# Value units read as halves of the contraction: 512-column matmuls into two banks, and another unit order in the memory layers

## The reference, cut to what matters

```python
# layer 0: vg is the gate input of the gated MLP, 512 columns
q, k, v, iq, ik, iw, u, vg = split_cols(h @ ab_w_in[e], AB_SPLITS)
y_b = gmlp_spatial_gate(gelu(u), gelu(vg), ...)
# layer 1: i are the values (1024 columns), gate the output gate (1024)
q, f, i, gate = split_cols(h @ c_w_in[o_i], C_SPLITS)
o = rms_norm(hgrn2(q, f, i, lb_all[l]), c_out_norm[o_i])
y = (o * silu(gate)) @ c_w_out[o_i]
# layers 2 and 3: q, k, v of 768 columns each, qm of 256
proj = xn @ w_in
self_out = attention(q, k, v);  mem_out = memory_attention(qm, mk, mv)
h = h + concat(self_out, mem_out) @ w_out[i]
```

## Time and profile before

| | us |
|---|---|
| median of 3 runs (lowest, highest) | 1290.58 (1290.05, 1291.75) |
| the profiled execution's own time | 1290.27 |
| its span, first to last instruction | 1288.5 |
| PE busy | 1272.3 |
| PE weight loads busy | 1127.0 |
| DVE busy | 991.9 |
| ACT busy | 751.0 |

### The profile page before, as it was taken

One profiled execution on the slowest core, in us unless ns is written; L12 is line 12 of the kernel. 1 busy time (PEld: TensorE's weight loads), 2 busy tenths in 40 slices (PEclk: granted clock), 3 DMA queues, 4 the chain that ended last, 5 costly groups with the idle time before them and its releaser, 6 DMA issues.

```text
span 1288.5 us, 21452 instructions
## 1 busy us (share of the span) xinstructions
PE 1272.3 (99%) x8114; PEld 1127.0 (87%) x8114; DVE 991.9 (77%) x1470; ACT 751.0 (58%) x1095; POOL 17.8 (1%) x34
## 2 busy tenths in 40 slices
PE   8999999999999999999999999999999999999998
PEld 7898888888999988888889888888889997888886
DVE  5898798888788778899987766777776675866665
ACT  5465665555877657776656656544445555644443
POOL 2000000000000001000000000000000000000000
PEclk9999999999999999999999999999999999999999
DMA  9554655556534347566546443655564444556551
GB/s 320 198 164 134 196 196 187 182 187 194 155 108 136 127 151 242 176 211 200 184 128 196 132 133 130 209 186 193 195 194 158 155 145 134 180 196 195 190 185 49
DMA packets 168918, 223.19 MB, mean 173 GB/s; under 512 B 5240, under 2 KB 150784, under 8 KB 168720
## 3 DMA queue, kind: packets, MB, share of 16 engines
q1 hardware_dynamic: 166480, 216.04, 51.4%
q0 software_dynamic: 1936, 5.54, 1.3%
q10 hardware_dynamic: 432, 0.64, 0.1%
HBM read 221.15 MB, written 1.06 MB: 172 GB/s over the span
## 4 chain that ended last, share of the span: by engine, by line
PE 86%; DVE 7%; ACT 3%; issue 2%; DMA 1%; DVEq 0%; SPq 0%; ACTq 0%
PE bank L547 21%; PE bank L385 16%; PE bank L386 15%; PE bank L387 15%; PE bank L550 11%; DVE wlow L1563 2%; PE bank L872 2%; ACT whigh L1105 1%; PE bank L641 1%; PE bank L677 1%; PE bank L663 1%; PE bank L462 1%; DMA raw<-in_ab_w_in 1%; DMA raw<-in_ffn_w_down 1%; DVE conv_b L1700 1%
## 5 line engine op out<-in xcount | busy, mean ns | idle before, releaser
L1563 DVE TENSOR_TENSOR wlow<-raw,whigh 128x2048 fp32r<-128x2048 f32 (+1 forms) x203 | 462.4, 2281 | 137.6 <-ACT whigh L1105 137.1
L1105 ACT ACTIVATE whigh<-raw 128x2048 fp32r<-128x2048 f32 x202 | 386.1, 1912 | 230.5 <-PE bank L387 148.4
L547 PE MATMUL bank<-xn,whigh 128*128 128x512 f32 x1312 | 327.9, 392 | 0.0
L547 PEld LDWEIGHTS bank<-xn,whigh 128*128 128x128 f32 x1312 | 238.2, 189 | 44.1
L550 PEld LDWEIGHTS bank<-xn,wlow 128*128 128x128 f32 x1312 | 179.0, 190 | 12.8
L550 PE MATMUL bank<-xn,wlow 128*128 128x256 f32 x1312 | 182.9, 282 | 0.0
L385 PE MATMUL bank<-xn,whigh 128*128 128x256 f32 (+1 forms) x560 | 161.8, 289 | 0.6 <-DVE wlow L1563 0.6
L386 PE MATMUL bank<-xn,whigh 128*128 128x256 f32 (+1 forms) x560 | 158.3, 283 | 0.0
L387 PE MATMUL bank<-xn,wlow 128*128 128x256 f32 (+1 forms) x560 | 158.2, 283 | 0.0
L385 PE MATMUL bank<-whigh,g_high 128*128 128x512 f32 x354 | 138.7, 392 | 1.7 <-DVE g_low L1759 1.0
L386 PE MATMUL bank<-wlow,g_high 128*128 128x512 f32 x354 | 137.8, 389 | 0.0
(11 more groups left out here) (292 smaller groups left out, 1756.1 us busy)
## 6 DMA issues: line engine op xcount, KB each, us to landing
raw<-in_ffn_w_up SPq DMA_DIRECT2D x44, 1024.0 KB, 5.1
raw<-in_w_gate_up SPq DMA_DIRECT2D x44, 1024.0 KB, 5.1
raw<-in_ffn_w_down SPq DMA_DIRECT2D x22, 1024.0 KB, 4.9
raw<-in_w_down SPq DMA_DIRECT2D x22, 1024.0 KB, 4.8
raw<-in_c_w_in SPq DMA_DIRECT2D x16, 1024.0 KB, 5.5
raw<-in_ab_w_in SPq DMA_DIRECT2D x14, 1024.0 KB, 7.1
raw<-in_w_in_fox SPq DMA_DIRECT2D x10, 1024.0 KB, 5.4
raw<-in_w_in_moba SPq DMA_DIRECT2D x10, 1024.0 KB, 5.1
```

The costliest lines, as they stand in the source:

```text
L547: pe.matmul(o[:, :].rearrange("p (h t) -> p h t", h=2), wh[:, k, j * P:(j + 1) * P], xn[:, :, k, :], start=k == 0, stop=False)
L1105: act.activation(whigh[s][:, 0:w], raw[s][:, 0:w], ACT.Copy).then_inc(w_high, 1)
L1563: dve.tensor_tensor(wlow[s][:, 0:w], raw[s][:, 0:w], whigh[s][:, 0:w].bitcast(F), ALU.subtract).then_inc(w_low, 1)
```

## The change

Twelve of the eighteen token-stationary units are joined in pairs: vg0 with vg1 in layer 0; i0 with i1, i2 with i3 and g2 with g3 in layer 1; v0 with v1 in layers 2 and 3. The first unit of a pair now holds contraction tiles 0 to 3 of 512 columns, the second tiles 4 to 7 of the same 512. A pair fills two banks, one for each token tile, over both units, and both are complete only in the second. ACT takes a pair with two instructions of 512 columns in the second unit, ahead of its `high`, where it took each unit with two of 256. The first unit's weights are released by a new semaphore, `half_used`. In layers 2 and 3 the order becomes q0 k0 v0 v1 q1 k1 q2 k2 v2, and the self pairs 2 and 3 start at s = 6 and 7, not 5 and 6. The four accumulators of layer 1's output projection lie in banks 1, 3, 2, 0, not 0, 1, 2, 3.

```diff
+    def half_rows(w, c0, half):
+        return [(tall(w, c0, 512)[:, KT // 2 * half:KT // 2 * (half + 1), :], 256)]
...
-    OUT_BANKS = {0: (0, 1, 6, 7), 1: (0, 1, 2, 3), 2: (0, 1, 6, 7), 3: (0, 1, 7, 6)}
+    OUT_BANKS = {0: (0, 1, 6, 7), 1: (1, 3, 2, 0), 2: (0, 1, 6, 7), 3: (0, 1, 7, 6)}
...
+    HGRN_PAIRED = (("i", 0), ("i", 1), ("i", 2), ("i", 3), ("g", 2), ("g", 3))
...
-    BEGIN = (0, 1, 2, 3, 5, 6, 8, 9)
+    BEGIN = (0, 1, 2, 3, 6, 7, 8, 9)
+    MIX_UNITS = [(name, int(n)) for name, n in "q0 k0 v0 v1 q1 k1 q2 k2 v2".split()]
...
+        def unit_half(u, name, banks, half, between=None):
+            fetched(u)
+            s = u % RING
+            wh = whigh[s][:, :].rearrange("p (k c) -> p k c", k=KT // 2)
+            wl = wlow[s][:, :].rearrange("p (k c) -> p k c", k=KT // 2)
+            for t in range(TT):
+                if t and between is not None:
+                    between()
+                if half == 0:
+                    fill(name + (t,), banks[t])
+                f = FILLS[name + (t,)]
+                for kk in range(KT // 2):
+                    k = KT // 2 * half + kk
+                    last = split3(psum[f.bank][:, :], xn_high[:, k, t * P:(t + 1) * P], xn_low[:, k, t * P:(t + 1) * P],
+                                  wh[:, kk, :], wl[:, kk, :], half == 0 and kk == 0, half == 1 and kk == KT // 2 - 1)
+                if half:
+                    last.then_inc(bank_full[f.bank], 1)
+            if half:
+                USED[u] = (bank_full[f.bank], f.now, 0)
+            else:
+                last.then_inc(half_used, 1)
+                halves[0] += 1
+                USED[u] = (half_used, halves[0], 0)
...
             emptied(("level", STEPS * p + 8))
-            emptied(("i", 1, p))
+            for t in range(TT):
+                emptied(("i", 1, "pair", p // 2, t))
...
+                if (name, j) in HGRN_PAIRED:
+                    if j % 2 == 0:
+                        pair_banks[0] = (bank4(), bank4())
+                    unit_half(FIRST[name, 1, j], (name, 1, "pair", j // 2), pair_banks[0], j % 2, between=between)
...
+        def pair_taken(name, dst, func=ACT.Copy):
+            for t in range(TT):
+                o, empty = full(name + (t,))
+                act.activation(dst[:, t, :], o[:, :], func, scale=rstd[:, t:t + 1]).then_inc(empty, 1)
...
             if u == 13:
                 heads_root(0, 2, 2)
+            if u < 16:
+                name, j = HGRN_UNITS[u]
+                if (name, j) in HGRN_PAIRED and j % 2:
+                    pair_taken((name, 1, "pair", j // 2), (h_i if name == "i" else h_gate)[:, :, 512 * (j // 2):512 * (j // 2 + 1)])
             if u < 19:
                 high(base + u + RING)
```

More of the change, by code:

```diff
@@ L332, in build @@
             segment(("f", l), columns(w, 3 * SELF, qm))
-        for j in range(3):
-            for n, name in enumerate(("q", "k", "v")):
-                segment((name, l, j), columns(w, n * SELF + 256 * j, n * SELF + 256 * (j + 1)))
+        for name, j in MIX_UNITS:
+            at_ = "qkv".index(name) * SELF + 256 * j
+            segment((name, l, j), half_rows(w, 2 * SELF, j) if name == "v" and j < 2 else columns(w, at_, at_ + 256))
         rows = A["w_out_2"][l - 2].rearrange("(f p) c -> p f c", p=P)
@@ L391, in _ @@
         ring = [0]
+        halves, pair_banks = [0], [None]
         def high_first(o, wh, wl):
@@ L813, in _ @@
                 name, j = AB_UNITS[u]
-                unit = unit_tokens if name in ("v", "vg") else unit_columns
-                unit(FIRST[name, 0, j], (name, 0, j), bank4(), xn_high, xn_low, between=values)
+                if name == "vg":
+                    if j == 0:
+                        pair_banks[0] = (bank4(), bank4())
+                    unit_half(FIRST[name, 0, j], (name, 0), pair_banks[0], j, between=values)
+                else:
+                    unit = unit_tokens if name == "v" else unit_columns
+                    unit(FIRST[name, 0, j], (name, 0, j), bank4(), xn_high, xn_low, between=values)
             if u == 1:
@@ L953, in _ @@
             for s in range(13):
-                name, n = "qkv"[s % 3], s // 3
+                name, n = MIX_UNITS[s] if s < 9 else (None, None)
                 def values():
@@ L964, in _ @@
                     out_unit(l, s - 9, 6 + 3 * (l - 2), accs, values)
+                elif name == "v" and n < 2:
+                    if n == 0:
+                        pair_banks[0] = (bank4(), bank4())
+                    unit_half(FIRST["v", l, n], ("v", l), pair_banks[0], n, between=values)
                 elif name == "v":
@@ L1425, in _ @@
                 act.activation(h_k[:, pair, :], h_g[:, pair, :], ACT.Identity, bias=1.0, scale=-1.0).then_inc(key_ready, 1)
-            if u < 16 and name in "ig":
+            if u < 16 and name in "ig" and (name, j) not in HGRN_PAIRED:
                 dst = h_i if name == "i" else h_gate
@@ L1490, in _ @@
                         high(FIRST["out", l] + s - 9 + RING)
+                elif name == "v" and n < 2:
+                    if n:
+                        pair_taken(("v", l), f_v[:, :, 0:512])
+                    high(FIRST["v", l, n] + RING)
                 elif name == "v":
```

36 lines of the change are left out of this document (20 added, 16 removed).

## The result

| | before | after |
|---|---|---|
| median, us (lowest, highest; runs) | 1291.27 (1290.05, 1292.54; 13) | 1293.90 (1292.68, 1295.57; 13) |
| the profiled execution's own time, us | 1290.27 | 1292.68 |
| its span, us | 1288.5 | 1290.9 |

The changed kernel is slower by 0.2%: the ratio is 1.0020, 95% interval 1.0013 to 1.0027. I had said 1290.4 us, 1287.0 to 1292.6. The measured time is 2.6 us above the kernel before, and 1.3 us above my range. The kernel before was itself 0.7 us above the 1290.58 us of three runs from which I had started.

The account below looks back on a forecast made before the run. PE was taken to bound the kernel, busy 1272.3 of 1288.5 us. 3.57 us gained and 3.39 lost made −0.2 us against 1290.27, thus 1290.1, and 1290.4 us for the median; range 1287.0 to 1292.6 us.

Parts of the forecast that it names:

- The stall in g2: Layer 1, middle of g2: PE waits 3.39 us (3.2 to 4.8) for bank 0, until ACT takes i2 and i3.
- ACT's chain move 1.04 us: Layer 1: DVE's start and ACT's chain up to the late take come 1.04 us earlier, 3.5 units at 0.30 us.
- nothing took the stall back: From g2 to the end of layer 1's output projection no PE wait absorbs the delay, so it passes on whole.
- i2 has no wait: Layer 1, middle of i2: `h_i` is ready with 0.5 us of slack; cost nothing, at worst 0.5 us.
- layer 0's table load stayed covered: Layer 0: the moved table load makes `vg_rms` about 1.15 us later, hidden by 1.7 us of slack before DVE's read.
- PE waits for no `f_pT` in layers 2 and 3: Layers 2 and 3, first value pair: copies ready with 0.6 us of slack; cost nothing, otherwise 0.5 us a layer.
- the fall of the clock to 1.2 GHz: Rival, 8%: behind the g2 stall PE's clock falls, 2.6 us more for 12 matmuls, 1293.0 us, or 1295.5 us if longer.
- 3.57 us of gain: All six pairs: 48 matmuls of 512 columns replace 96 of 256, 0.60 us a pair, all on PE's path.
- My rival of a smaller gain: Rival, 4%: 512-column matmuls cost nearly twice 256-column ones, leaving the stall alone, at most 1294.0 us.
- the Trainium skill's 2.5 ns for each matmul: All pairs: by this fixed part 48 fewer matmuls save 0.12 us a pair, 0.7 us in all; case then about 1293.3 us.
- My fast rival: Rival, 13% on the fast side: the whole gain of 3.57 us without the g2 stall, 1287.0 us.

Follow-up runs that it names:

- PE kept busy: Changed kernel with the 12 matmuls of g2's first row tile computed once more behind the levels, output the same; 1292.35 us, ratio 1.0008 to the kernel before.
- the early take: Changed kernel with ACT's take of pair i2, i3 moved right behind the square of heads 1, ahead of exponentials, table load and root; 1288.04 us, ratio 0.9973 to before.
- the root last: Changed kernel with the root of heads 0 and 1 and its table load behind the take of pair i2, i3; 1292.11 us, ratio 0.9999 to before.
- the levels behind: Against the changed kernel: take of i2, i3 early, and layer 1's mid-unit levels in paired units moved behind both row tiles; 1293.74 us, ratio 1.0017 to before.
- the memory layers as before: Changed kernel with the take of i2, i3 early and layers 2 and 3 undone (order, starts, single value units); 1288.93 us, ratio 0.9985 to before.

## Why the prediction was wrong, by its own steps

**The stall in g2 was right, in place and cause, and in its length.** I had a wait of 3.39 us, counted from the earliest start of the second tile, and that start came 3.37 us late (3.18 in the trace's own count, which ends the levels' record later). The clock times agree as well, but by luck. I forecast 445.88 us for the start and 442.49 for PE's arrival, and they were 445.69 and 445.69 − 3.37 = 442.32. These times leave out the 0.5 us that layer 0 is shorter, and they take 0.34 us too much for the gain of nine groups; the two errors nearly cancel. I had ACT's chain move 1.04 us with PE. Its table load came 444.77 − 443.47 = 1.30 us earlier; less layer 0's 0.5, that is 0.8, or seven groups at 0.11. The other parts held: nothing took the stall back, i2 has no wait, layer 0's table load stayed covered, and PE waits for no `f_pT` in layers 2 and 3.

**The step that failed first is the stall's price: I took the wait alone.** I named the fall of the clock to 1.2 GHz as a rival, priced it at 2.6 us for 12 matmuls, and gave it 8%. It happened: the group took 4.44 us against 2.84, so 1.6 us, less than 2.6 because only seven of the twelve distances are 0.42 to 0.43 us. The kernel with PE kept busy shows that the idling did it. I had written that no wait of that length was in the trace, and put the chance low for that reason; a missing example should have left it open, not made it unlikely. The Trainium skill ("TensorE: Matmul & The Clock Gate", section "What's actually happening") says that an idle TensorE goes to 1.2 GHz until it has been busy again; the trace of the change agrees, with a granted clock of 0.53 and 0.62 behind 3.18 us of waiting. Not every wait here did that (last section).

**The second is a term mis-sized: of 3.57 us of gain, the paired layers show about 2.4.** I priced all six pairs by distances from runs without a break. For vg, which runs so, 0.60 became 0.61. In layer 1 each pair is cut into four groups of twelve, and a group gains 0.11 us, not 0.15: 1.3 us, not 1.8. In each memory layer the marks of before and after show 0.25 us where I had 0.60, and 0.2 to 0.6 over all traces; how much of that the edges of the groups take was not tried. 0.6 + 1.3 + 0.5 = 2.4. The medians cannot confirm that the whole gain is so much smaller. The kernel with the early take is 3.6 us under before, with an interval of 2.2 to 4.7, which holds 2.4 and 3.57. In its trace the first column is 0.84 us shorter, of which vg's pair is 0.61, and ffn 1 is 0.88 shorter; whether the change has a part in the rest is not shown. My rival of a smaller gain had almost none of it left, 1294.0 us. That is near the measured 1293.9 by luck: most of the gain is there, and the clock took it back. By the Trainium skill's 2.5 ns for each matmul ("TensorE: Matmul & The Clock Gate", section "Wait — 56ns, not 53.3ns?") vg's pair would have saved 0.12 us, an estimate, and the trace, 0.61, does not agree for these operands.

Together, for the profiled executions: +1.6 us of clock and +1.2 us of gain not there, less 0.3 us in ffn 1, make about 2.5 of the 2.6 us between my 1290.1 and its 1292.68. The median lies 1.2 us higher still, since no execution of the thirteen was faster than the profiled one, where I had added 0.3. The three slowest, 1295.3 to 1295.6 us, have a mean clock of 0.995 and the fastest 0.998, so more slow stretches than the traced one are likely a part of that; no trace shows them.

**The version to keep** is the change with the early take: 1288.04 us, 0.27% under the kernel before, where the change as made is 0.20% above it. My fast rival, 1287.0 us, was this kernel: the gain without the stall. It lies 1.0 us above that because the kernel before, timed beside it, had 1291.68 us and not 1290.58. Its 3.6 us under before are the rival's 3.57, with 0.9 us of them in ffn 1, which I had not counted.

## What to carry to other kernels

When work units are paired so that two buffers are held over both, list who releases each of them and what stands ahead of that release on its engine. Here two lines of order on an engine that was 58% busy decided between 0.2% slower and 0.3% faster. Price a wait of TensorE as itself plus the slow stretch that may follow it: here that was 1.6 us, behind waits of 1.57 and 3.18 us. And take a saving per matmul from runs that are as long as those the kernel will have: here each group behind levels costs 0.12 us extra with 512 columns and 0.08 with 256, which took 0.04 of 0.15 us.

## What the hardware showed that I had not expected

**The length of a wait does not decide alone whether the clock falls.** Two waits for a copy of `h_i`, 1.57 us in the kernel with the root last and 1.55 us in the one with the levels behind, ended differently. The second, in PE's timeline and windows:

```profile
423.47 0.50 PE L392 MATMUL bank<-whigh,xn 128*128 128x512 f32 x1 [1.55 <-ACT h_i L1213]
423.81 0.40 PE L393 MATMUL bank<-wlow,xn 128*128 128x512 f32 x1
```

```profile
422.00:424.00 2.00, 0.53 (x2) 1.00 0.62 241
424.00:426.00 2.00, 2.00 (x10) 1.00 0.03 8
```

Here the clock stayed up; in the kernel with the root last it was 0.50 in the windows 444 to 446. And a wait that every kernel has, before and after, near 38.8 us in layer 0 (1.05 us for `rel_tab`), left the clock at 1.00 in the trace of before,

```profile
38.00:40.00 2.00, 1.16 (x9) 1.00 0.08 27
40.00:42.00 2.00, 2.00 (x17) 1.00 0.35 69
```

but not in that of the kernel with the memory layers as before (0.76, 0.50 and 0.89 in these windows), nor in that with layer 1 as before:

```profile
38.00:40.00 2.00, 1.23 (x8) 0.84 0.08 29
40.00:42.00 2.00, 2.00 (x10) 0.50 0.37 57
42.00:44.00 2.00, 2.00 (x16) 0.80 1.02 379
```

That is the same program up to there, in another execution. It goes with the long first columns of those two, 147.99 and 148.00 us.

Behind its first matmul PE waits 27 times for 1.0 us or more in the eleven traces. The clock fell behind five of these waits: 3.18 us in the changed kernel, 2.53 in the one with layer 0's pair alone, 1.57 with the root last, and two of the eleven of 1.05 us. It stayed up behind the others, of which the longest are 2.35 and 2.34 us.

The mean granted clock of each execution points the same way, though it is a blunt measure: each trace also has 2 to 4 us at half clock at the end of the kernel, 0.0007 to 0.0015 of it, where it costs nothing (from the last feed-forward matmul to the end all eleven take 24.3 us). Of 31 runs of the kernel before, 19 at 0.998 average 1292.06 us and 12 at 0.999 average 1291.02. The average over the executions is 0.9968 for the changed kernel (3.18 us of waiting), 0.9973 with the root last (1.57 us), and 0.9985 and 0.9987 with PE kept busy and with the early take. A slow stretch is worth 0.0013. So behind the wait of 3.2 us the clock fell in most executions, and behind 1.57 us in many but not all. What in an execution decides it was not tried and stays open.
